# The first stage of a two-block layer stack, reordered: x in halves, weights ahead of the modulation, two rows of its first part on TensorE

## The reference, cut to what matters

```python
mod = (silu(c) @ ada_w + ada_b).reshape(bsz, DEPTH, 2, 3, D_MODEL)     # 12288 columns
shift, scale, gate = mod[:, 0, 0, 0], mod[:, 0, 0, 1], mod[:, 0, 0, 2]
h = rmsnorm(x, norm_g[0, 0]) * (1.0 + scale) + shift
b_gate, c_gate, v = split(h @ a_w_in, 3)                                # 1024 x 3072
y = (b_gate * causal_conv(c_gate * v)) @ a_w_out
x = x + gate * rmsnorm(y, norm_g[0, 1])
# then a SwiGLU layer, a Mamba-2 layer (it needs dt_bias, a_log), a second SwiGLU,
# and the second block: windowed and selected attention, a merge, a conv FFN, a last norm
```

## Time and profile before

| | us |
|---|---|
| three executions | 2267.8, 2261.09, 2255.58 (median 2261.09) |
| the profiled execution | 2257.73 |
| its span, first to last instruction | 2255.9 |
| PE busy | 2185.6 |
| DVE, ACT, POOL busy | 1229.8, 993.5, 975.6 |
| mean granted clock of PE | 0.982 |

### The profile page before, as it was taken

One profiled execution on the slowest core, in us unless ns is written; L12 is line 12 of the kernel. 1 busy time (PEld: TensorE's weight loads), 2 busy tenths in 40 slices (PEclk: granted clock), 3 DMA queues, 4 the chain that ended last, 5 costly groups with the idle time before them and its releaser, 6 DMA issues.

```text
span 2255.9 us, 28975 instructions
## 1 busy us (share of the span) xinstructions
PE 2185.6 (97%) x10440; PEld 1758.1 (78%) x10440; DVE 1229.8 (55%) x1722; ACT 993.5 (44%) x1420; POOL 975.6 (43%) x421
## 2 busy tenths in 40 slices
PE   6999999999999999989999999999999899999998
PEld 4788888888877777767788888878677688888886
DVE  5776765521277777787522221250778755666412
ACT  4324543334445546544534333453555644444332
POOL 3444444346634324334544446556211143444563
PEclk8999999999999999999999999999999999999999
DMA  7553475553315334333233323334221032332232
GB/s 310 211 206 126 153 275 202 184 151 93 116 50 196 126 122 154 113 111 94 66 102 93 93 75 98 115 101 151 95 69 48 29 106 81 103 101 93 77 93 73
DMA packets 74193, 273.88 MB, mean 121 GB/s; under 512 B 8615, under 2 KB 11303, under 8 KB 67832
## 3 DMA queue, kind: packets, MB, share of 16 engines
q1 hardware_dynamic: 70728, 266.77, 36.3%
q10 hardware_dynamic: 3376, 5.90, 0.8%
HBM read 269.24 MB, written 8.12 MB: 123 GB/s over the span
## 4 chain that ended last, share of the span: by engine, by line
PE 76%; issue 14%; POOL 5%; DVE 3%; ACT 1%; DMA 0%; ACTq 0%; POOLq 0%; SPq 0%; DVEq 0%
PE bank L545 60%; POOL wlo L506 5%; PE bank L921 4%; PE bank L568 2%; PE bank L1014 2%; PE bank L978 1%; PE bank L942 1%; PE bank L572 1%; PE bank L961 1%; PE bank L656 1%; PE bank L617 1%; PE bank L609 1%; PE bank L862 1%; DVE x L1561 0%; DMA x<-x_d 0%
## 5 line engine op out<-in xcount | busy, mean ns | idle before, releaser
L506 POOL TENSOR_TENSOR wlo<-raw,whi 128x1024 fp32r<-128x1024 f32 x382 | 930.2, 2442 | 1195.7 <-ACT whi L1052 1195.6
L1052 ACT ACTIVATE whi<-raw 128x1024 fp32r<-128x1024 f32 x382 | 400.9, 1055 | 580.4 <-PE bank L545 549.8
L545 PE MATMUL bank<-h_hi,whi 128*128 128x512 f32 x1616 | 639.7, 396 | 5.1 <-DVE tb L1660 3.3
L545 PE MATMUL bank<-h_hi,wlo 128*128 128x512 f32 x1616 | 634.2, 392 | 0.0
L545 PE MATMUL bank<-h_lo,whi 128*128 128x512 f32 x1616 | 632.5, 391 | 0.0
L545 PEld LDWEIGHTS bank<-h_hi,whi 128*128 128x128 f32 x1616 | 304.0, 188 | 75.2 <-issue 9.7
L545 PEld LDWEIGHTS bank<-h_hi,wlo 128*128 128x128 f32 x1616 | 303.8, 188 | 66.8
L545 PEld LDWEIGHTS bank<-h_lo,whi 128*128 128x128 f32 x1616 | 304.0, 188 | 65.0
L545 PE MATMUL bank<-g_lo,whi 128*128 128x512 f32 x592 | 232.2, 392 | 0.0
L545 PE MATMUL bank<-g_hi,wlo 128*128 128x512 f32 x592 | 232.1, 392 | 0.0
L545 PE MATMUL bank<-g_hi,whi 128*128 128x512 f32 x592 | 230.9, 390 | 0.0
(11 more groups left out here) (343 smaller groups left out, 2930.9 us busy)
## 6 DMA issues: line engine op xcount, KB each, us to landing
raw<-f_in_d SPq DMA_DIRECT2D x88, 512.0 KB, 3.6
raw<-m_d SPq DMA_DIRECT2D x65, 512.0 KB, 3.7
ada_f<-ada_d SPq DMA_DIRECT2D x24, 1024.0 KB, 6.5
raw<-g_in_d SPq DMA_DIRECT2D x44, 512.0 KB, 3.5
raw<-w_in_d SPq DMA_DIRECT2D x41, 512.0 KB, 3.6
csb<-cs_d SPq DMA_DIRECT2D x32, 640.0 KB, 6.5
ada_a<-ada_d SPq DMA_DIRECT2D x16, 1024.0 KB, 4.9
raw<-a_in_d SPq DMA_DIRECT2D x24, 512.0 KB, 5.9
```

What stands on the lines that cost most here:

```text
L506: nc.gpsimd.tensor_tensor(wlo[:, s], raw[:, s], whi[:, s].bitcast(F32), ALU.subtract).then_inc(lo_ready, 1)
L545: mm = nc.tensor.matmul(psum[bank][:], w[:, s, kk, :], xs[part == "lo"][:, k, :], start=first and kk == 0 and i == 0, stop=last and kk == ...
L1052: nc.scalar.activation(whi[:, s], raw[:, s], ACT.Copy).then_inc(hi_ready, 1)
```

## The change

1. SP's order: `vec`, x in two halves with a semaphore each, `kst`, chunks 0 and 1, part 0, chunks 2 and 3, parts 1 to 3, `dtp` with a semaphore of its own, `tbl`, `hot`.
2. ACT waits for each half of x before its first square, splits chunk 0 behind square 6 and chunk 1 behind square 7, chunk 2 behind `set_root` and chunk 3 behind the root.
3. Rows 6 and 7 of part 0 (`DIRECT`) are no longer multiplied by DVE: `first_sum(0)` on PE multiplies `ada_first` with the silu columns directly, eight one-column matmuls, and adds DVE's six rows to them.
4. `first_sum(1)`, (2), (3) come behind turns 1, 3 and 5 of `four` instead of before it and behind turns 1 and 3. In turn 0 PE waits for the residue of each chunk by itself instead of for all four.
5. DVE does the first half of part 1 behind `scaled` 0 and 1, instead of before `ssum`.
6. The two later readers of `dtp` wait for its own semaphore.

```diff
@@ sync
             sp.dma_start(vec[:], io["vec"]).then_inc(vec_in, 16)
+            for h in range(2):
+                sp.dma_start(x[:, 4 * h:4 * h + 4], io["x"].rearrange("p (k n) -> p k n", k=KD)[:, 4 * h:4 * h + 4]).then_inc(x_in[h], 16)
             sp.dma_start(kst[:], io["kst"]).then_inc(kst_in, 16)
-            sp.dma_start(dtp[:].rearrange("p a h -> p (a h)"), io["dtp"].broadcast_to([P, 2 * HEADS])).then_inc(kst_in, 16)
-            sp.dma_start(x[:], io["x"].rearrange("p (k n) -> p k n", k=KD)).then_inc(x_in, 16)
+            for v in range(2):
+                load(io["a_in"][v], v)
             ada_start(0)
-            ada_start(1)
-            for v in range(4):
+            for v in range(2, 4):
                 load(io["a_in"][v], v)
-            ada_start(2)
-            ada_start(3)
+            for p in range(1, 4):
+                ada_start(p)
+            sp.dma_start(dtp[:].rearrange("p a h -> p (a h)"), io["dtp"].broadcast_to([P, 2 * HEADS])).then_inc(dtp_in, 16)
@@ tensor, four
                     for i in which:
+                        if k == 0:
+                            pe.wait_ge(lo_ready, C0[name] + i + 1)
                         high(i, k)
...
-                pe.wait_ge(lo_ready, C0[name] + 4)
                 for k in range(KD - 2):
                     turn(k, range(4))
-                    if n == 0 and k in (1, 3):
-                        first_sum(2 + k // 2)
+                    if n == 0 and k % 2:
+                        first_sum(1 + k // 2)
@@ tensor, first_sum
-                pe.wait_ge(mod_part, p + 1)
                 if p:
                     pe.wait_ge(mod_out, p)
+                else:
+                    pe.wait_ge(csil_ready, 1)
+                    pe.wait_ge(first_in[0][1], 16)
+                    for k in DIRECT:
+                        for b in range(4):
+                            nc.tensor.matmul(first_bank(0)[:, b:b + 1], ada_first[0][:, k, b * P:(b + 1) * P], csil[:, k:k + 1],
+                                             start=k == DIRECT[0] and b == 0, stop=False, skip_group_check=True)
+                pe.wait_ge(mod_part, p + 1)
                 for b in range(4):
...
             first_sum(0)
-            pe.wait_ge(kst_in, 32)
+            pe.wait_ge(kst_in, 16)
             spread(4, 0, R1)
-            first_sum(1)
             four("a_in", 0)
@@ scalar
-            act.wait_ge(x_in, 16)
             act.wait_ge(const_ready, 1)
             for k in range(KD):
+                if k % 4 == 0:
+                    act.wait_ge(x_in[k // 4], 16)
                 if k >= 2:
                     act.wait_ge(row_done, k - 1)
                 nc.scalar.activation(sq[:, k % 2, :], x[:, k, :], ACT.Square).then_inc(sq_out, 1)
+                if k >= KD - 2:
+                    split_hi(k - (KD - 2))
             act.wait_ge(row_done, KD)
             nc.scalar.activation(rstd[0:1, :], psum[4][0:1, :], ACT.Copy).then_inc(row_out, 1)
             set_root()
+            split_hi(2)
             act.wait_ge(s_ready, 1)
             take_root(0, ssum[:])
-            for c in range(RING):
-                split_hi(c)
+            split_hi(3)
             mod_norm(0, "a_in", 0)
@@ vector, first_part: DIRECT = (6, 7)
-                for k in range(max(1, half * h), half * (h + 1)):
+                end = KD if p else DIRECT[0]
+                for k in range(max(1, half * h), min(half * (h + 1), end)):
@@ vector
             for p in range(4):
-                if p < 3:
+                if p in (1, 2):
                     first_part(p + 1, 0)
...
                 for k in range(2 * p, 2 * p + 2):
                     scaled(k, 4, 0, "a_in")
+                if p == 0:
+                    first_part(1, 0)
                 if p < 3:
                     first_part(p + 1, 1)
```

More of the change, by code:

```diff
@@ L237, in program @@
         in_hi, in_ready = sem("in_hi"), sem("in_ready")
-        x_in, vec_in, kst_in, const_ready, csil_ready, out_ready, out_done = (
-            sem(n) for n in ("x_in", "vec_in", "kst_in", "const_ready", "csil_ready", "out_ready", "out_done"))
+        vec_in, kst_in, dtp_in, const_ready, csil_ready, out_ready, out_done = (
+            sem(n) for n in ("vec_in", "kst_in", "dtp_in", "const_ready", "csil_ready", "out_ready", "out_done"))
+        x_in = [sem("x_in0"), sem("x_in1")]
         first_in = [[sem(f"first_in{p}_{h}") for h in range(2)] for p in range(4)]
@@ L339, in roots @@
             return 1 + 2 * r + i
+        DIRECT = (6, 7)
         X_SUM = {0: 14, 1: 15}
@@ L659, in first_sum @@
             def first_sum(p):
-                pe.wait_ge(mod_part, p + 1)
                 if p:
                     pe.wait_ge(mod_out, p)
+                else:
[6 more added lines that the diff above has]
+                pe.wait_ge(mod_part, p + 1)
                 for b in range(4):
                     mm = nc.tensor.matmul(first_bank(p)[:, b:b + 1], (modacc, acc)[p % 2][:, b * P:(b + 1) * P],
-                                          ones[:, 0:1], start=True, stop=True)
+                                          ones[:, 0:1], start=p > 0, stop=True, skip_group_check=p == 0)
                 mm.then_inc(mod_sum, 1)
@@ L1189, in _ @@
             split_hi(C0["m_in"] + RING)
-            act.wait_ge(kst_in, 32)
+            act.wait_ge(dtp_in, 16)
             nc.scalar.activation(psum[6][:, 0:HEADS], dtp[:, 1, :], ACT.Exp).then_inc(a_exp, 1)
@@ L1621, in first_part @@
                     dve.wait_ge(mod_sum, p - 1)
-                for k in range(max(1, half * h), half * (h + 1)):
-                    ins = STT(out=out if k < KD - 1 else (modacc, acc)[p % 2][:], in0=ada_first[p][:, k, :], scalar=csil[:, k:k + 1],
+                end = KD if p else DIRECT[0]
+                for k in range(max(1, half * h), min(half * (h + 1), end)):
+                    ins = STT(out=out if k < end - 1 else (modacc, acc)[p % 2][:], in0=ada_first[p][:, k, :], scalar=csil[:, k:k + 1],
                               in1=out, op0=ALU.mult, op1=ALU.add)
-                    if k < KD - 1:
+                    if k < end - 1:
                         step(ins)
@@ L1763, in _ @@
             done(C0["m_in"])
-            dve.wait_ge(kst_in, 32)
+            dve.wait_ge(kst_in, 16)
+            dve.wait_ge(dtp_in, 16)
             b = T0["m_in"] % 4
```

## The result

The changed kernel took 2266.19 us in the median of 13 executions (2262.43 to 2268.16), the kernel before 2260.01 in 13 (2255.58 to 2267.8). The ratio is 1.0021, with a 95% interval of 1.0012 to 1.0030: 4.7 us slower (0.0021 x 2260; the two medians alone lie 6.2 apart, still inside that interval). That is clear of noise and within the 0.5% that the prediction called no change; 2263 was forecast, +2.4. The profiled execution took 2266.29, its span is 2264.4.

The account below looks back on a forecast made before the run. PE, 97% busy and nearly dense behind the first stage, was taken as the bound. `four` would end 1.9 us earlier without the clock, which costs 4.3: +2.4, 2263.0 on the mean of runs, range 2254 to 2270.

Parts of the forecast that it names:

- B: Rival: in `four` the clock holds through the stops, 1.9 us faster, 2258.6; chance 0.22.
- C: Rival: in `four` the clock stays low for 6 us behind each stop, +6.5 us, 2267; chance 0.20.
- the 60 to 67 that was named as a sign: Sign at the end of the first stage: `four` ends between 60 and 67 us.
- That the profile before is dense behind the stage, so the end of `four` is the measure.: Behind the first stage PE is nearly dense, so a microsecond won or lost at the start carries to the end.
- Transfers: Start of kernel: with `dtp` moved back, x's halves land at 6.2 and 8.7 us; 2.4 later if `dtp` isn't the cause.
- Sums of squares, splits: ACT and PE before `four`: sums of squares end at 17.4 us instead of 22.64.
- Two rows on PE: Sum 0 before `four`: ready at 21.95 us; the two rows cost 0.6 rather than gain 1.6.
- To the first turn: From sum 0 to `four`: `scaled(0)` at 23.8 us, `four` starts at 25.25, 10.07 earlier than before.
- The ring: In `four`: turns, sum, columns and `scaled`, `h_hi`, next turns; PE stops 1.9 us behind each of three sums.
- The clock: In `four`: granted clock falls behind each of three stops, 1.6 us each, 4.3 in all after 0.5 for hidden residue waits.
- D: Rival: PE begins `four` at 25.25 and stays dense, keeping the whole 10 us, 2250.5; chance 0.05.
- E: Rival: x's halves bring nothing, start only 4 us earlier, end up to 6 later than forecast, 2269; chance 0.03.

Follow-up runs that it names:

- run 4: Changed kernel with the sums at their old places (sum 1 ahead of `four`, 2 and 3 behind turns 1 and 3); ratio 1.0009 to the kernel before.
- run 9: run 1's kernel with two more unused 512-column matmuls as padding behind `four`; ratio 1.0006 to the kernel before.
- run 11: Kernel before with thirteen unused 512-column matmuls as padding behind `four`; ratio 1.0013 to the kernel before.
- run 12: run 6's kernel with the inverse of the root ahead of part 0's columns on DVE instead of behind them; ratio 0.9982 to the kernel before.
- run 2: Changed kernel with sums 1, 2, 3 behind turns 0, 2 and 4 of `four` instead of 1, 3 and 5; ratio 0.9999 to the kernel before.
- run 3: Kernel before with only the sums moved, 1, 2, 3 now behind turns 1, 3 and 5 of `four`; ratio 1.0057 to the kernel before.
- run 5: Changed kernel with all eight rows of part 0 on DVE, no direct products on PE; ratio 1.0043 to the kernel before.
- run 6: Changed kernel with all eight rows of part 0 on DVE and the sums behind turns 0, 2 and 4; ratio 0.9998 to the kernel before.
- run 8: Changed kernel with the transfer of `dtp` back ahead of x, behind vec; ratio 1.0049 to the kernel before.
- run 10: run 6's kernel with six unused 512-column matmuls as padding behind `four`; ratio 1.0002 to the kernel before.
- run 1: Changed kernel with eight extra unused 512-column matmuls behind each of sums 1 to 3, so PE works in the stops; ratio 1.0022 to the kernel before.
- run 7: Changed kernel with five extra unused 512-column matmuls in each stop, where run 1 has eight; ratio 1.0029 to the kernel before.

## Why the prediction was right

The mechanism forecast is the one that came: an earlier start, eaten up by three stops and three falls of the clock. The size was half of what came: +2.4 forecast, 4.95 measured in the stage and 4.7 in the time. The range of 2254 to 2270 would have held almost any outcome, B and most of C included; the rows, not the time, decide between them. The end of `four`, at 67.05, is just outside the 60 to 67 that was named as a sign.

**That the profile before is dense behind the stage, so the end of `four` is the measure.** The change itself agrees (4.95 in the stage, 4.7 timed), but the experiments show that luck was in it. The time lost beyond the stage, in us (ratio less one, times 2260, less the shift of the end of `four`), is within about 1 of zero for the change and for runs 4, 9, 11 and 12, 1 to 3.5 for runs 2, 3, 5, 6, 8 and 10, and 5 and 6 for runs 1 and 7. It was never clearly below zero. So the step holds to some 3 us in most kernels, and fails in two of the three with matmuls in the stops; only part of the reason was found (run 7).

**Transfers.** The first square came at 6.54 (6.2 was the forecast landing), DVE's part 0 began at 14.51 (14.1), and run 8 shows `dtp` as the cause of the slow stretch.

**Sums of squares, splits.** They end at 17.0 (17.4).

**Two rows on PE.** Sum 0 was ready at 21.9, as computed (21.95), partly by luck: PE began the direct products at 18.65 instead of 19.1, the clock fell at 20.1 and the sum took 1.45 instead of 0.95 (and the terms named, 19.1, 2.1 and 0.95, add up to 22.15). The cost of 0.6 was nearly right for sum 0 itself (0.4, run 6 against run 2), but not for what it is worth: undoing it cost 1.5 in the stage (run 5). What was missed is DVE's column waiting for POOL's residue, and the clock falling this early.

**To the first turn.** 25.25 forecast, 26.57 measured, 1.3 late: the spread of the root took 2.04 at the low clock, against 1.13 at the full one before, which the step "25.37 to 27.20, the same now" left out, and the column 0.39. The prediction had the clock low for the first pair of turns, but at the full rate for sum 0 and the spread ahead of it.

**The ring.** Three stops of 1.9 forecast; 2.14, 2.01, 1.94 measured. Runs 2 and 3 show the order of the sums as their cause. This is the step that decided the sign.

**The clock.** Three falls forecast at 1.6 each; three fell, two of 3.4 us and one of 6.8. Run 1 gives their price together: 5.0 at the end of `four`, 5.3 counted from the start of sum 1 (34.58 there, 34.29 in the changed kernel), against 4.3. That 1.0 and the 1.3 at the first turn are 2.3 of the 2.5 us by which the stage came out longer than forecast (4.95 against 2.4). The stops were 0.4 longer together and the first pair 0.85 shorter (7.7 for 8.55); about 0.6 us in the later pairs and the last turns isn't broken down. With the clock held (run 1) the stage ends 0.1 before that of the kernel before, where the sum without the clock had 1.9.

**Rivals.** B (the clock holds) falls by the rows, C (low for 6 us each time) holds for one stop of three, D (the gain of the start is kept) falls: `four` was no longer dense. E (the halves of x bring nothing) falls: the first square came at 6.54.

## What to carry to other kernels

When a stage is made to start earlier, look at what the early engine will wait for then: here 8.75 us of earlier start turned into 5 of later end, because each sum was put behind the second of two turns, right in front of the turn that needs what follows from it. Put the small step on which another engine hangs ahead of work that can cover the round trip (turn 0, sum, turn 1), not behind it: that took 8.2 us off the stage and 5 off the time. And price a stop on TensorE at the stop plus what the clock takes afterwards: here 6 us of stops cost 5 more in the stage.

## What the runs showed of the hardware that was not expected

A VectorE instruction with two inputs in SBUF and two numbers a partition (the scale column) took 0.36 to 2.08 us instead of 0.16 each of the thirteen times in these profiles that a GpSimd residue was in hand when it began, and ended 0.01 to 0.03 us behind that residue. With none in hand it took 0.16 every time in the stage. Instructions with one input in SBUF and one in PSUM (0.16 for the columns of `mod`, 1.28 for two scaled tiles) and the inverse (0.18 in run 12) were not held. The Trainium skill, "SBUF — State Buffer", SBUF: two separate sides, has this: VectorE and GpSimd share a pair of ports, locked for a whole instruction, and a VectorE op with two SBUF inputs wants it against a GpSimd op that reads SBUF. The runs agree, and show what it does to a chain of short steps: taking the inverse out from behind the column ended the stage 0.9 us earlier (run 12).

Where the granted clock falls and how long it stays low behind a sparse stretch differed between kernels by up to 7 us of low clock at the same place of the program (625 to 632). So a change in one stage can come with 4 us elsewhere, and a single profile of this kernel says little on sizes under that. The timed medians of five rounds do better, but they too differ from what the stage did by up to 6 us (run 7). What fixes those places is open, and so is whether they are fixed for a kernel or differ from one execution to the next: only one execution of each was profiled.
